# First-kind mixers: the halves of a rotation swapped by DMAs instead of a matmul, with three buffers

## The reference

```
cq, k_att, v_att, k_idx, w_idx, q_m, k_m, v_m, o_m, i_m, f_m = split(h @ w_in)
cq    = rms_norm(cq, q_latent_norm)
q     = rope(cq @ w_q_up)            # 8 heads of 64
q_idx = rope(cq @ w_qidx_up)         # 8 heads of 64
k     = rope(k_att);  k_idx = rope(k_idx)
score = sum_h relu(q_idx . k_idx) * w_idx ; keep the 128 best keys of each query, then softmax attention
q_m, k_m = split(silu(causal_dwconv(concat(q_m, k_m), conv_w, conv_b)))
ig = i_m + b_igate ; lf = log_sigmoid(f_m + b_fgate)     # the gates' rows
hm = mlstm_chunkwise(q_m, k_m, v_m, ig, lf)

rope(x): x1, x2 = halves of each head's 64 ; [x1*cos - x2*sin, x2*cos + x1*sin]
```

## Time and profile before

| what | value |
|---|---|
| median of 3 runs | 3579.34 us (3579.05 to 3589.06) |
| the profiled execution | 3599.26 us, span 3597.5 us |
| PE busy | 3309.4 us (92%) |
| DVE, ACT, POOL busy | 1539.9, 1325.5, 1314.6 us (43%, 37%, 37%) |
| DMA | 306 MB, 25.2% of 16 engines' span |
| granted TensorE clock, mean | 0.917 |

### The profile page before, as it was taken

The page is one execution under the profiler, slowest core; times in us unless marked ns, Lnnn a source line. Parts: engine busy times, 40 slices in busy tenths (PEclk is TensorE's granted clock), DMA queues, the critical chain, the costliest instruction groups (busy, mean ns, idle before and its releaser), DMA issues. The chain is left out here.

```text
span 3597.5 us, 39551 instructions
## 1 busy us (share of the span) xinstructions
PE 3309.4 (92%) x14840; PEld 2622.7 (73%) x14840; DVE 1539.9 (43%) x2474; ACT 1325.5 (37%) x2598; POOL 1314.6 (37%) x1118
## 2 busy tenths in 40 slices
PE   4987889998998899999998988999999989789998
PEld 3655768886666688877887766888778877668886
DVE  6686366604774442115003553553150036545521
ACT  3334432233435422333233633433332336244332
POOL 2332235543330344444440232444444402334443
PEclk8998899999999899999795888999998959899999
DMA  5123146621120132222310021332223200212222
GB/s 203 59 100 135 36 146 240 214 97 65 65 71 13 59 102 95 94 88 82 100 65 1 1 82 51 102 97 94 94 77 100 71 1 1 82 62 96 100 93 72
DMA packets 84719, 306.02 MB, mean 85 GB/s; under 512 B 9392, under 2 KB 9648, under 8 KB 84400
## 3 DMA queue, kind: packets, MB, share of 16 engines
q1 hardware_dynamic: 84528, 303.49, 25.2%
HBM read 301.36 MB, written 2.10 MB: 84 GB/s over the span
## 5 line engine op out<-in xcount | busy, mean ns | idle before, releaser
L174 POOL TENSOR_TENSOR wl<-raw,wh 128x512 fp32r<-128x512 f32 (+1 forms) x952 | 1248.2, 1315 | 1830.6 <-ACT wh L166 1828.9
L166 ACT ACTIVATE wh<-raw 128x512 fp32r<-128x512 f32 (+1 forms) x952 | 589.1, 623 | 1559.1 <-PE bank L188 1446.7
L186 PE MATMUL bank<-hh,wh 128*128 128x512 f32 x2624 | 1060.8, 404 | 84.9 <-DVE hl L436 60.6
L187 PE MATMUL bank<-hl,wh 128*128 128x512 f32 x2624 | 1036.9, 395 | 0.0
L188 PE MATMUL bank<-hh,wl 128*128 128x512 f32 x2624 | 1035.8, 395 | 0.0
L186 PEld LDWEIGHTS bank<-hh,wh 128*128 128x128 f32 x2624 | 502.6, 192 | 231.4 <-DVE hl L436 67.2
L187 PEld LDWEIGHTS bank<-hl,wh 128*128 128x128 f32 x2624 | 502.4, 191 | 109.2 <-issue 6.7
L188 PEld LDWEIGHTS bank<-hh,wl 128*128 128x128 f32 x2624 | 501.7, 191 | 107.7
L188 PE MATMUL bank<-hidh,wl 128*128 128x512 f32 x704 | 280.9, 399 | 0.0
L187 PE MATMUL bank<-hidl,wh 128*128 128x512 f32 x704 | 277.4, 394 | 0.0
L186 PE MATMUL bank<-hidh,wh 128*128 128x512 f32 x704 | 276.0, 392 | 0.0
(11 more groups left out here) (331 smaller groups left out, 3977.6 us busy)
## 6 DMA issues: line engine op xcount, KB each, us to landing
raw<-in_w SPq DMA_DIRECT2D x444, 512.0 KB, 3.4
mod_raw2a<-in_wmod SPq DMA_DIRECT2D x40, 512.0 KB, 4.5
mod_raw2b<-in_wmod SPq DMA_DIRECT2D x28, 512.0 KB, 4.7
raw<-in_w SPq DMA_DIRECT2D x32, 384.0 KB, 3.0
first_mods<-in_wmod SPq DMA_DIRECT2D x16, 512.0 KB, 13.5
rmod<-in_wmod SPq DMA_DIRECT2D x12, 512.0 KB, 4.1
x<-in_x SPq DMA_DIRECT2D x1, 2048.0 KB, 14.9
out_xT<-x SPq DMA_DIRECT2D x4, 512.0 KB, 2.6
```

Of the source, the lines that this page charges most:

```text
L166: act.activation(self.m.wh[:, t % 2, w_], self.m.raw[:, t % RING, w_], ACT.Copy)\
L174: pool.tensor_tensor(self.m.wl[:, t % 2, w_], self.m.raw[:, t % RING, w_], self.m.wh[:, t % 2, w_].bitcast(F32), ALU.subtract)\
L186: pe.matmul(out, wh, xh, start=start, stop=False)
L187: pe.matmul(out, wh, xl, start=False, stop=False)
```

## The change

Rotation r now goes so. DVE writes bank times cosines straight to the destination and bank times signed sines to one of three buffers `sines`; then the bank is free. SP waits for that and issues four DMAs of 32 partitions by 512 elements (64 KB each), which put the product's halves exchanged into one of three buffers `turns_`. DVE adds it to the destination two rotations later (`rope_end`). ACT's copies, PE's matmuls and their tables are gone. SP issues the swaps between the weight loads, in the loop over tiles. The sines carry the sign: `side`, a column of +1 and -1, is made once by DVE in the prelude, as the row sums of the permutation in `cst`, and is the scale of the Sin activation. Rotations 9 to 12 are all in DVE's tile 10. The copy `wi_col` moves from tile 9 to tile 10, and the six operations on the gates' rows from tile 9 to tile 13. The second kind of mixer keeps its matmuls.

```
+    def swap_halves(sp, dst, src, sem):
+        for at in range(0, P, 64):
+            sp.dma_start(dst[at:at + 32], src[at + 32:at + 64]).then_inc(sem, 16)
+            sp.dma_start(dst[at + 32:at + 64], src[at:at + 32]).then_inc(sem, 16)
...
+        sines = rawb[:, 0, :], rawb[:, 1, :], qk[:, 6, :]
+        turns_ = m.tmp[:, 0, :], m.tmp[:, 1, :], qk[:, 7, :]
-        RAW_AT = {3: (0,), 4: (1,), 5: (2, 3, 4, 5), 6: (6,), 7: (7,), 8: (8,), 9: (9, 10, 11, 12)}
-        TURN_MID = {6: 2, 7: 4, 8: 6, 9: 8, 10: 9, 11: 11}
-        TURN_END = {4: 0, 5: 1, 6: 3, 7: 5, 8: 7, 10: 10, 11: 12}
+        ROPE_TILE = (3, 4, 5, 5, 5, 5, 6, 7, 8, 9, 9, 9, 9)
+        rope_at = {4: (0,), 5: (1,), 6: (2, 3), 7: (4, 5), 8: (6, 7), 9: (8,), 10: (9, 10, 11, 12)}
...  sync
                 s.loads(sp, t0 + RING + t, t0 + RING + t + 1)
+                for r in rope_at.get(t, ()):
+                    sp.wait_ge(sine_ready, r + 1)
+                    if r >= 3:
+                        sp.wait_ge(rope_done, r - 2)
+                    swap_halves(sp, turns_[r % 3], sines[r % 3], swapped_in[r % 3])
...  tensor
-            def rotate(r):
-                pe.wait_ge(unrotated_ready, r + 1)
-                pe.matmul(ps[ropes[r][0]][:], rot, rawb[:, r % 2, :], start=True, stop=True)\
-                  .then_inc(rotated_ready, 1)
...  scalar
-                for r in RAW_AT.get(t, ()):
-                    if r >= 2:
-                        act.wait_ge(rope_done, r - 1)
-                    act.activation(rawb[:, r % 2, :], ps[ropes[r][0]][:], ACT.Copy).then_inc(unrotated_ready, 1)
...  vector
             def rope(r):
                 bank, dst = ropes[r]
+                s.done(dve, t0 + ROPE_TILE[r])
+                if r >= 3:
+                    dve.wait_ge(swapped_in[r % 3], 64 * (r // 3))
+                dve.tensor_tensor(dst, ps[bank][:], m.cos[:], ALU.mult)
                 freed[bank] += 1
+                dve.tensor_tensor(sines[r % 3], ps[bank][:], m.sin[:], ALU.mult).then_inc(sine_ready, 1)
+                dve.wait_ge(sine_ready, r + 1)
+                dve.sem_inc(bank_free[bank], 1)
+                if r >= 2:
+                    rope_end(r - 2)
+
+            def rope_end(r):
+                dst = ropes[r][1]
+                dve.wait_ge(swapped_in[r % 3], 64 * (r // 3 + 1))
+                dve.tensor_tensor(dst, dst, turns_[r % 3], ALU.add).then_inc(rope_done, 1)
+                dve.wait_ge(rope_done, r + 1)
...
-                if t == 9:
+                if t == 10:
                     dve.wait_ge(wi_turned, 1)
                     dve.tensor_copy(wi_col, ps[0][:, 0:32]).then_inc(bank_free[0], 1)
                     dve.wait_ge(bank_free[0], 3)
+                if t == 11:
+                    rope_end(ROPES - 2)
+                    rope_end(ROPES - 1)
+                if t == 13:
                     dve.wait_ge(gate_log, 1)
                     ... the six operations on the gates' rows, unchanged
...  prelude
+            act.wait_ge(side_set, 1)
             act.activation(idle4, m.eps[:, 0:1].to_broadcast([P, 4]), ACT.Sqrt)
...
             dve.memset(m.eps[:, 1:2], 0.0).then_inc(eps_set, 1)
+            dve.wait_ge(cst_in, 16)
+            dve.tensor_reduce(side, rot, AX_X, ALU.add).then_inc(side_set, 1)
             dve.wait_ge(c_act, 1)
```

More of the change, by code:

```diff
@@ L238, in build @@
     idle4 = m.col[:, 40:44]
+    side = m.col[:, 44:45]
     def mod(l, i):
@@ L670, in build @@
     M1_SEMS = tuple(f"bank_free{b}" for b in range(8)) + (
-        "latent_sq", "latent_sum", "latent_root", "latent_ready", "unrotated_ready", "rotated_ready", "rope_done",
+        "latent_sq", "latent_sum", "latent_root", "latent_ready", "sine_ready", "swapped_in0", "swapped_in1", "swapped_in2", "rope_done",
         "conv_base", "conv_done", "ones_set", "reduced", "rope_order", "order", "act_order",
@@ L685, in first_mixer @@
         bank_free = sems[0:8]
-        (latent_sq, latent_sum, latent_root, latent_ready, unrotated_ready, rotated_ready, rope_done,
+        (latent_sq, latent_sum, latent_root, latent_ready, sine_ready, swapped_in0, swapped_in1, swapped_in2, rope_done,
          conv_base, conv_done, ones_set, reduced, rope_order, order, act_order,
@@ L693, in first_mixer @@
          summed, root_in, root, ascaled, aturned, ahead, late_ready) = sems[8:]
-        mod_in = mod_in0, mod_in1
+        mod_in, swapped_in = (mod_in0, mod_in1), (swapped_in0, swapped_in1, swapped_in2)
+        sines = rawb[:, 0, :], rawb[:, 1, :], qk[:, 6, :]
+        turns_ = m.tmp[:, 0, :], m.tmp[:, 1, :], qk[:, 7, :]
         kinds = MIX1_KINDS
@@ L700, in first_mixer @@
         ropes[0] = (3, ki[:])
[L701 to L703 removed]
+        ROPE_TILE = (3, 4, 5, 5, 5, 5, 6, 7, 8, 9, 9, 9, 9)
+        ROPES = len(ropes)
+        rope_at = {4: (0,), 5: (1,), 6: (2, 3), 7: (4, 5), 8: (6, 7), 9: (8,), 10: (9, 10, 11, 12)}
         iitems = [(tb, h) for tb in range(1, NT) for h in range(HEADS)]
@@ L819, in tensor @@
                                 last.then_inc(s.slot_done[k], 1)
-                        if nb == 1 and t in TURN_MID:
-                            rotate(TURN_MID[t])
                 else:
@@ L926, in scores @@
                 elif i < 2:
+                    pe.wait_ge(rope_done, ROPES)
                     claim(i)
@@ L1012, in scalar @@
                     act.wait_ge(reduced, 2)
-                    act.activation(m.sin[:], m.sin[:], ACT.Sin).then_inc(reduced, 1)
+                    act.activation(m.sin[:], m.sin[:], ACT.Sin, scale=side).then_inc(reduced, 1)
                     act.activation(m.cos[:], m.cos[:], ACT.Sin).then_inc(reduced, 1)
@@ L1138, in rope @@
                 bank, dst = ropes[r]
-                dve.wait_ge(unrotated_ready, r + 1)
-                step(dve.tensor_tensor(m.tmp[:, 0, :], rawb[:, r % 2, :], m.cos[:], ALU.mult))
-                dve.wait_ge(rotated_ready, r + 1)
+                s.done(dve, t0 + ROPE_TILE[r])
+                if r >= 3:
+                    dve.wait_ge(swapped_in[r % 3], 64 * (r // 3))
+                dve.tensor_tensor(dst, ps[bank][:], m.cos[:], ALU.mult)
                 freed[bank] += 1
-                dve.tensor_tensor(m.tmp[:, 1, :], ps[bank][:], m.sin[:], ALU.mult).then_inc(bank_free[bank], 1)
-                dve.wait_ge(bank_free[bank], freed[bank])
-                dve.tensor_tensor(dst, m.tmp[:, 0, :], m.tmp[:, 1, :], ALU.add).then_inc(rope_done, 1)
+                dve.tensor_tensor(sines[r % 3], ps[bank][:], m.sin[:], ALU.mult).then_inc(sine_ready, 1)
[7 more added lines that the diff above has]
+                dve.tensor_tensor(dst, dst, turns_[r % 3], ALU.add).then_inc(rope_done, 1)
                 dve.wait_ge(rope_done, r + 1)
@@ L1339, in first_mixer @@
         return stage
-    PRE_SEMS = ("x_in", "cst_in", "c_in", "c_act", "p_in", "pc_in", "pos_in", "eps_set", "order") + tuple(
+    PRE_SEMS = ("x_in", "cst_in", "c_in", "c_act", "p_in", "pc_in", "pos_in", "eps_set", "side_set", "order") + tuple(
         f"cols_in{j}" for j in range(4))
@@ L1345, in prelude @@
     def prelude(sems, jun):
-        x_in, cst_in, c_in, c_act, p_in, pc_in, pos_in, eps_set, order, *cols_in = sems
+        x_in, cst_in, c_in, c_act, p_in, pc_in, pos_in, eps_set, side_set, order, *cols_in = sems
         def sync(sp):
```

5 lines of the change are left out of this document (removed).

## The result

The changed kernel takes 3561.95 us (median of 6, 3561.05 to 3571.32), the kernel before beside it 3579.52: ratio 0.995, 95% interval 0.9934 to 0.9966. Measured twice more, it gave 0.9938 (0.992 to 0.9956; 3556.4 against 3583.7) and 0.9938 (0.9915 to 0.9961; 3566.6 against 3582.5). The kernel before against itself gave 1.0005 (0.9992 to 1.0017). So the gain is 16 to 27 us by the medians and 18 to 22 by the ratios; 21.7 were forecast. (A ratio is always to the kernel before, timed beside the kernel named.

What follows compares the result with a forecast made beforehand. PE was taken to bound the first-kind mixers until tile 14, then DVE and ACT together. First mixer -9.3 and second -12.4 make -21.7 us off the median 3579.34: 3557.6 us, range 3551 to 3571, chance 0.76.

Steps and rivals of the forecast that it cites:

- The rotations: PE, both first-kind mixers: rotations 1 to 12 save 0.87 us each, 10.4 us; with two waits gone, 12.6 us a mixer.
- Rotation 0 in the second mixer: PE at the second mixer's start: of its 0.87 us some 0.4 is gained, as the latent is ready at 890.97.
- The gates' rows: DVE, tile 13: six operations of 5.2 us make its taps 2.1 to 3.5 us late; after slack, 0.6 us a mixer.
- Rival (a): DVE has no slack in tile 13, so the gates cost 6.6 us per mixer, not 0.6; 3569.6 us; chance 0.10.
- The swaps: SP's four DMAs per rotation: 3.6 us from product to landed, needed after 4.4 us; no wait, 0.8 us to spare.
- wrong altogether: Sign of failure: swaps landing after more than 6 us, or PE meeting a new wait between tiles 5 and 17.
- The two readings of the Trainium skill's pages: Swaps: four transfers wholly behind one another take 9.3 us; with the fixed part overlapped, 3.3 us.
- (b): Swaps go one by one, some 9.4 us from product to landed; lead 4.3 us per mixer, 3573 us; chance 0.07.
- (c): Swaps queue behind other traffic; slower from about 11 us on; with a 13.5 us landing, 3589 us; chance 0.04.
- The prelude: Before the first mixer: DVE waits for cst and begins 12.0 us later; 2.7 us paid, between 1.3 and 3.6.
- Rival (d): DVE alone sets the mixer's end, so PE's lead is not taken over; nothing gained, about 3583 us; chance 0.03.
- no clock is priced: Whole kernel: no clock change counted, since the waits before 88.6 and at 203 us are there in both kernels.

Runs made afterwards that it cites:

- Tile 15: The changed kernel with the gates' six row operations in tile 15 instead of 13: 3582.09 us, ratio 0.9981 to the kernel before.
- the dummies: The changed kernel with 12 dummy matmuls of a rotation matmul's shape per first-kind mixer, in tiles 6, 7, 8, 10 and 11: 3588.39 us, ratio 1.001.

## Why the prediction was right, step by step

**The rotations.** Right in kind, low in size. I had 0.87 us each from one spacing; put back, they cost 0.89 to 0.95. With the two waits of 0.74 and 1.38 us, which did go, that makes 12.8 to 13.5 us a mixer, and 12.8 to 13.8 were measured where I had 12.6 less the gates' 0.6. The error of this term is 0.4 to 1.8 us over both mixers. One attribution in it was wrong: the wait of 1.38 us was due to the gates' six operations, which stood ahead of the sine product that ends it in DVE's list (rotation 11's, ending at 144.25; I had written 10's). Moving them alone takes it away, and with them back in tile 9 the changed kernel has a wait of 1.57 us. The sum is not touched by this, only what earned it. Rotation 0 in the second mixer was worth 0.1 to 0.4 us (from the end of the SwiGLU block to tile 5: 52.42 and 52.19 us before, 52.07 to 52.09 after), where I had 0.4.

**The gates' rows.** They last 5.1 us, as estimated from their unstretched neighbours, and not 6.6. Tile 13's taps come 10.43 us after tile 12's, 2.1 late as forecast (8.32 is the beat there), and tile 14's at 160.19 = 143.22 + 8.32 + 8.64: not late at all. So the term is 0 and not 0.6, and with the 1.1 to 1.9 us that the move earns in tile 9 it is a gain. Tile 15 shows the edge of that slack: 6.0 and 5.2 us. Rival (a) is dead for tile 13 and true for tile 15.

**The swaps.** The conclusion held (no wait that counts), the price did not. An issue takes SP 0.51 to 0.60 us and not the 0.33 of an isolated load, and even the weight load among them takes 0.58. A set that finds SP free costs about what I wrote: the fourth issue starts 1.8 to 1.9 us after the first and lands 2.0 later, 3.8 us against 3.6. What I left out is the queue. Between 104 and 118 us SP is still issuing the set before or a weight load when the next product is ready, and a swap issued right behind a weight load lands late (up to 3.9 us). So from the first issue to the last landing a set of the first mixer took 3.8 to 4.9 us, and from the product's end to the last landing 3.8 to 7.4 us, over 6 in four of the 13 rotations; rotation 6, shown above, is the 7.4 (108.96 to 116.34). By my own list more than 6 us was a sign of being "wrong altogether". That sign was met and the forecast held, so it was set too tight: DVE reached rotation 6's sum 6.2 us after its product and not the 4.4 that I had between two rotations. DVE waited 1.2, 0.8 and 0.5 us in three places, with no bracket on PE for any of them. That it came out at no cost was in part luck: the margin of 0.8 us was used up, and the run with the sums one late shows what was at stake. The two readings of the Trainium skill's pages (DMA: Bandwidth & Descriptors, Rules for kernel authors; SBUF — State Buffer, The DMA setup-cost knee) come apart here. Each transfer landed 1.9 to 3.9 us after its issue, about 2.0 where nothing was queued ahead, which is the fixed cost of about 2 us that the second page gives. But the fixed costs overlapped: a set took 3.8 to 4.9 us, far from four of them in a row, and rivals (b), with 9.4 us, and (c), from 11 us on, are out. Whether the bytes of the four go one after another this doesn't tell, since their issues lie 0.6 us apart.

**The prelude.** +1.5 us where I had +2.7. DVE began at 22.50, 0.16 later than `cst` had been there before, as forecast, and the reduction took 0.29. But the idle time was absorbed to the end, and of the last four blocks only one was stretched much (1.34 and 2.27 us); three had been (1.96, 2.27 and 2.27). DVE's reciprocal was 3.2 us late (36.45 against 33.23) and the end of the blocks 1.5. My lower bound (1.3) was the right end. ACT's part was hidden, as written: its norm is done at 34.99, and DVE's reciprocal starts at 36.45 straight behind its twelfth block. (The run that hides the reduction removes ACT's wait as well, so it can't tell the two apart.)

**Who sets the pace.** PE up to tile 13, then DVE with PE within half a microsecond a tile, then DVE's list up to the first weights. I had read the change of hands at tile 14 from the brackets and drew from it that PE's lead is carried on; the attention started 12.7 us earlier in the first profile (325.94 against 338.63). Rival (d) is out. PE's wait before tile 18 did not grow to 7, as it had to if the gates cost 0.6; it stayed at 6.38.

**The total.** The stretches give 25 to 26 us, 21.7 were forecast; the ratios give 18 to 22. The near hit of 3557.6, with medians of 3561.95, 3556.4 and 3566.59, is therefore partly luck: each mixer gained some 1.4 us more and the prelude cost 1.2 less than I wrote, which is 3 to 4 us too little forecast, and the granted clock took about as much back in the groups measured. My sentence that no clock is priced, because the waits are the same in both kernels, left out two things. The mean granted clock of the changed kernel's 18 executions is 0.9213 and that of the kernel before in the later groups 0.9223 to 0.9227, worth some 2 us at 20 us for 0.01; by the executions' own spread that difference is hardly beyond noise. And the spread itself is 10 us between the medians of one kernel, nearly half of the gain. A slip in the range: gates free, prelude 1.3 and lead 13 give 3554.2 and not 3555, which changes nothing.

**What it adds up to.** Of the 12.8 to 13.8 us of a mixer the dummies account for 10.7 to 11.4 (PE's matmuls), the gates' move for 1.1 to 1.3, and the wait for POOL, which vanished with ACT's copies, for 0.7: 12.5 to 13.4 in all. The last is read from the two traces; no run took away ACT's copies alone.

## What to carry to other kernels

- If a stretch shows one engine without a single bracket, an operation taken from it is worth its spacing in full; check the worth by putting dummies of the same shape back.
- A list that is handed through several engines has a tile behind which every added microsecond is paid: find it by the engine whose bracket names the other, and put loose work one tile ahead. Work that waits for a two-buffer stream belongs between other work, one by one: that alone gave 8 us here, all of it in the first mixer.
- Judge changes of under 10 us by stretches between fixed points in the trace, with the granted clock beside them, not by the medians alone.

## What was not expected of the hardware

- Issuing a transfer costs SP 0.51 to 0.60 us in a dense row of transfers within SBUF, even for a weight load among them, against 0.33 in the kernel before; one issue took 1.31 us. From 104 to 118 us SP issues almost without a gap: it is close to being a bound.
- A 64 KB transfer within SBUF landed about 2.0 us after its issue where nothing was queued ahead, and up to 3.9 us where a weight load of 512 KB had been issued just before its set (rotation 9's, issued from 120.68 us behind the load at 119.99). Four of them overlapped: 3.8 us for a set, not 8.
- A DVE sum of 128x512 from two SBUF operands takes 0.69 us alone, and 1.16 to 1.76 us in 6 of the 13 sums of a mixer (the second time measured). All six begin or run while POOL is in one of its 128x512 subtractions (those at 97.42, 103.47, 111.70, 119.18, 123.15 and 125.79 us); of the other seven, five lie outside them. Each of the six ends 0.53 to 0.56 us after the end of one subtraction (the first at 100.51, POOL's pair at 99.96; the last at 127.64, POOL's at 127.08), as if the sum had waited for it. One more, at 109.42, lies inside POOL's pair from 108.40 on and took only 0.82, but there POOL's two took 3.00 us instead of 2.54. That the two engines hold each other up is argued from these times; no run took POOL's work away.
- The same kernel, at the same point to 0.6 us, was given a clock of 0.89 or 0.53 over 30 us of its attention.
